# Gating the down weights instead of the sums in four modulated FFNs of a ten-stage fp32 block

## What is computed

```python
mod = (silu(c) @ w_mod[i] + b_mod[i]).reshape(-1, 3, 3, D)
h = modulate(x, norm_g[i, 0], mod[:, 0, 0], mod[:, 0, 1])
x = x + 0.5 * mod[:, 0, 2][:, None, :] * ((silu(h @ w_gate) * (h @ w_up)) @ w_down)
```

## Time and profile before

| | before |
|---|---|
| median of three runs | 2032.69 us |
| the profiled execution's own time | 2035.07 us |
| its span, first to last instruction | 2033.0 us |
| TensorE busy (matmul) | 1890.1 us, 93% |
| VectorE busy | 1424.8 us, 70% |
| ScalarE busy | 1173.2 us, 58% |
| HBM read | 371 MB, 183 GB/s over the span |
| granted TensorE clock, mean | 0.970 of full speed |

### The profile page before, as it was taken

One profiled execution on the slowest core, in us unless ns is written; L12 is line 12 of the kernel. 1 busy time (PEld: TensorE's weight loads), 2 busy tenths in 40 slices (PEclk: granted clock), 3 DMA queues, 4 the chain that ended last, 5 costly groups with the idle time before them and its releaser, 6 DMA issues.

```text
span 2033.0 us, 35938 instructions
## 1 busy us (share of the span) xinstructions
PE 1890.1 (93%) x14638; PEld 1737.6 (85%) x14638; DVE 1424.8 (70%) x2154; ACT 1173.2 (58%) x2049; POOL 12.9 (1%) x25
## 2 busy tenths in 40 slices
PE   6898899898989998999899999999989997889998
PEld 6887899887769997999889867899989996868998
DVE  5686877754667777877687676777787776565555
ACT  5544656664666556565576675555565555554332
POOL 0000000020000000000000000000000000000000
PEclk9999999989989998999999999899999998989999
DMA  8303666255057654888334403688778863124551
GB/s 318 115 4 120 221 231 238 94 188 186 23 182 252 238 212 165 324 290 286 131 136 162 150 1 121 252 289 287 242 263 291 285 228 125 53 93 156 187 187 52
DMA packets 96179, 374.96 MB, mean 184 GB/s; under 512 B 5776, under 2 KB 6416, under 8 KB 95248
## 3 DMA queue, kind: packets, MB, share of 16 engines
q1 hardware_dynamic: 95376, 372.15, 51.2%
q10 hardware_dynamic: 640, 0.52, 0.1%
HBM read 371.08 MB, written 1.05 MB: 183 GB/s over the span
## 4 chain that ended last, share of the span: by engine, by line
PE 84%; DVE 9%; ACT 5%; issue 2%; DMA 0%; ACTq 0%; DVEq 0%; SPq 0%
PE psum L997 36%; PE psum L1013 17%; PE psum L696 8%; PE psum L783 5%; PE psum L980 2%; PE psum L526 2%; DVE buf L597 2%; PE psum L1620 1%; PE psum L654 1%; DVE htok L2887 1%; PE psum L2997 1%; PE psum L3445 1%; PE psum L2505 1%; DVE x_res L490 1%; DVE htok L489 1%
## 5 line engine op out<-in xcount | busy, mean ns | idle before, releaser
L997 PEld LDWEIGHTS psum<-buf,buf 128*128 128x128 f32 x6048 | 741.9, 192 | 9.3
L997 PE MATMUL psum<-buf,buf 128*128 128x256 f32 x6048 | 745.7, 283 | 0.0
L1013 PE MATMUL psum<-buf,buf 128*128 128x512 f32 x1584 | 383.6, 391 | 2.2 <-DVE buf L1062 2.2
L1013 PEld LDWEIGHTS psum<-buf,buf 128*128 128x128 f32 x1584 | 289.2, 188 | 57.9 <-DVE buf L1062 3.0
L895 DVE TENSOR_TENSOR buf<-ring,buf 128x1024 fp32r<-128x1024 f32 x264 | 311.2, 1220 | 10.7 <-DVE modT L951 7.5
L889 ACT ACTIVATE buf<-ring 128x1024 fp32r<-128x1024 f32 x264 | 263.2, 1046 | 5.2 <-DVE buf L769 4.1
L696 PE MATMUL psum<-buf,buf 128*128 128x256 f32 x1944 | 245.9, 286 | 8.9 <-DVE buf L597 8.4
L696 PEld LDWEIGHTS psum<-buf,buf 128*128 128x128 f32 x1944 | 237.8, 192 | 14.6 <-DVE buf L597 13.1
L911 DVE TENSOR_TENSOR buf<-ring,buf 128x1024 fp32r<-128x1024 f32 x132 | 161.7, 1225 | 86.2 <-ACT buf L906 86.2
L906 ACT ACTIVATE buf<-ring 128x1024 fp32r<-128x1024 f32 x132 | 139.4, 1056 | 87.7 <-PE psum L1013 85.2
L597 DVE TENSOR_TENSOR buf<-ring,buf 128x1024 fp32r<-128x1024 f32 x97 | 118.7, 1232 | 92.6 <-ACT buf L591 85.3
(11 more groups left out here) (430 smaller groups left out, 2070.8 us busy)
## 6 DMA issues: line engine op xcount, KB each, us to landing
ring<-in_w_ffn SPq DMA_DIRECT2D x88, 1536.0 KB, 6.8
buf<-in_w_mod SPq DMA_DIRECT2D x144, 512.0 KB, 4.6
ring<-in_w_conv SPq DMA_DIRECT2D x44, 1536.0 KB, 6.5
ring<-in_w_ssd_in SPq DMA_DIRECT2D x16, 1536.0 KB, 6.4
ring<-in_w_hy_in SPq DMA_DIRECT2D x7, 1536.0 KB, 18.9
ring<-in_w_ns_in SPq DMA_DIRECT2D x7, 1536.0 KB, 7.4
ring<-in_w_ssd_out SPq DMA_DIRECT2D x5, 1536.0 KB, 6.6
ring<-in_w_cmp SPq DMA_DIRECT2D x4, 1024.0 KB, 5.2
```

The costliest lines, as they stand in the source:

```text
L997: ins = E.matmul(b[:, g * T:(g + 1) * T], w[:, wa, g, k, :], h[:, ha, k, :], start=k + n_ == 0, stop=k == KC - 1 and n_ == 2)
L1013: ins = E.matmul(acc[:, t, g * 512:(g + 1) * 512], hr[z][:, ha, t * P:(t + 1) * P], wd[z][:, wa, g * 512:(g + 1) * 512], start=j == 0 and ...
```

## The change

The gate is no longer multiplied into the sums. In the four modulated FFNs VectorE multiplies the raw down weights of each round by `rowb` (new function `gate_down`, into two new buffers `gated`), and the split works on the product. The row is made ahead of the first split. At the end VectorE only adds the sums to x. The cast of the hidden block goes from VectorE to ScalarE in these four FFNs. The conv FFNs are as they were. `pe_down` waits for `down_split` by name, and no longer for the row.

```diff
+        def add_plain(done):
+            ...
+                for t in range(NT):
+                    V.wait_ge(*done[t])
+                    added.append(dve.count(V.tensor_tensor(x[:, t, :], x[:, t, :], acc[:, t, :], ALU.add).then_inc(dve.sem, 1)))
...
+            gated = [Region(R_AT + 20480 + 4096 * u).take(CHUNK) for u in range(2)]
+            gated_at, high_at = {}, {}
...
+            def gate_down(j, row_point):
+                s, full = slot[j]
+                @block.vector
+                def _(_e):
+                    V.wait_ge(*full)
+                    V.wait_ge(*row_point)
+                    Ring.row_free = gated_at[j] = dve.count(V.tensor_tensor(gated[j % 2], slot_ap(s, SLOT)[:, 2 * CHUNK:], rowb[:, :],
+                                                                            ALU.mult).then_inc(dve.sem, 1))
...
             def split_down(j, free):
-                raw = slot_ap(s, SLOT)[:, 2 * CHUNK:]
+                raw = slot_ap(s, SLOT)[:, 2 * CHUNK:] if gate is None else gated[j % 2]
...
+                    if gate is not None:
+                        A.wait_ge(*gated_at[j])
                     Ring.p = act.count(A.activation(wd[j % 2][:, 0, :], raw, ACT.Copy).then_inc(act.sem, 1))
...
                     E.wait_ge(*hid[j])
-                    if j == 0 and gate is not None:
-                        E.wait_ge(*row_point)
+                    E.wait_ge(*down_split[j])
...
-                    vl(V.tensor_copy(hr[z][:, 0, :], hf[z]).then_inc(dve.sem, 1))
+                if gate is None:
+                    @block.vector
+                    def _(_e):
+                        vl(V.tensor_copy(hr[z][:, 0, :], hf[z]).then_inc(dve.sem, 1))
+                else:
+                    @block.scalar
+                    def _(_e):
+                        A.wait_ge(*mult[j])
+                        if j >= 2:
+                            A.wait_ge(*down[j - 2, 1])
+                        high_at[j] = act.count(A.activation(hr[z][:, 0, :], hf[z], ACT.Copy).then_inc(act.sem, 1))
+
+                @block.vector
+                def _(_e):
+                    if gate is not None:
+                        V.wait_ge(*high_at[j])
...
                 up_zero(h_pts)
+                if gate is not None:
+                    row_point = gate_row(mod_col(*gate, 2), 0.5, 0, [h_pts[-1]])
+                    gate_down(0, row_point)
                 split_down(0, [h_pts[-1]])
                 if gate is not None:
-                    row_point = gate_row(mod_col(*gate, 2), 0.5, 0, [h_pts[-1]])
+                    gate_down(1, row_point)
                 mod_products(0)
...
                     split_down(j, [down[j - 2, 1]] if j >= 2 else [h_pts[-1]])
+                    if gate is not None and j + 1 < NF:
+                        gate_down(j + 1, row_point)
...
-                add = add_normed if gate is None else add_gated
-                return add([down[NF - 1, 0], down[NF - 1, 1]], row_point), (bias if len(mods) else None)
+                ends = [down[NF - 1, 0], down[NF - 1, 1]]
+                return add_normed(ends, row_point) if gate is None else add_plain(ends), (bias if len(mods) else None)
```

More of the change, by code:

```diff
@@ L491, in add_gated @@
             return added
+        def add_plain(done):
+            added = []
+            @block.vector
[3 more added lines that the diff above has]
+                    added.append(dve.count(V.tensor_tensor(x[:, t, :], x[:, t, :], acc[:, t, :], ALU.add).then_inc(dve.sem, 1)))
+            return added
         def norm_transpose(gain, shift, added, parts, bias=None):
@@ L999, in _, with pe_down @@
                     up[j] = pe.count(ins.then_inc(pe.sem, 1))
-            def pe_down(j, row_point):
+            def pe_down(j):
                 z = j % 2
@@ L1096, in run @@
                     mod_sums(j - 1)
-                    pe_down(j - 1, row_point)
+                    pe_down(j - 1)
                     split_down(j, [down[j - 2, 1]] if j >= 2 else [h_pts[-1]])
+                    if gate is not None and j + 1 < NF:
+                        gate_down(j + 1, row_point)
                     if nxt is not None and j == NF - 4:
@@ L1109, in run @@
                     load_table(ACT.Sqrt)
-                pe_down(NF - 1, None)
+                pe_down(NF - 1)
                 def bias():
                     add_bias()
-                add = add_normed if gate is None else add_gated
-                return add([down[NF - 1, 0], down[NF - 1, 1]], row_point), (bias if len(mods) else None)
+                ends = [down[NF - 1, 0], down[NF - 1, 1]]
+                return add_normed(ends, row_point) if gate is None else add_plain(ends), (bias if len(mods) else None)
             return dict(load_a=load_a, load_b=load_b, pre_a=pre_a, pre_b=pre_b, run=run, gain=gain, shift=shift, h=h)
```

## The result

The changed kernel takes 2049.92 us in the median (2048.48 to 2053.63, four runs) against 2032.62 beside it: a ratio of 1.0090, 95% interval 1.0077 to 1.0103. It is slower by 17.3 us. The forecast was 2054, with a range of 2045 to 2067. A second set of runs beside the experiments gave 2051.96 against 2032.39, 1.0093 (1.0078 to 1.0108). The profiled execution took 2053.63 us, its span is 2051.5.

The account below looks back on a forecast made before the run. TensorE was taken as the bound, with 84% of the chain that ended last. Losses of 29.1 us less 8.2 gained gave net +20.9 on the median of 2032.69, forecast 2054 us, range 2045 to 2067.

Parts of the forecast that it names:

- The start: First rounds of each FFN: VectorE waits for the row, `up(2)` 7.1 us later in three FFNs, 2.8 in FFN 11.
- The round: Settled rounds with two side rows: VectorE's chain 8.47 us, taken as 8.50, equal to TensorE's; its slack falls to nothing.
- The tail: End of each FFN: one add per half without gate multiplies gains 2.2, 1.5, 2.2 and 2.35 us, 8.2 in all.
- The sum: All four FFNs: lost 9.3 + 8.5 + 8.5 + 2.8 = 29.1 us, gained 8.2, net +20.9.
- The signs of being wrong: Settled rounds: L1058 following L1058 by over 8.6 us, or TensorE waiting for VectorE in the middle of an FFN.
- The clock at the start: Rival: gaps at FFN starts lower TensorE's clock in `up(2)`, 0 to 3 us more, 2054 to 2057; no chance of its own.
- The long loop: Rival: VectorE's settled round exceeds TensorE's, priced at 8.65 to 8.70 us, 2064 us; range 2058 to 2076, chance 0.20.
- The faster case: Rival: FFN start costs under 2 us, `hid(0)` ready by about the end of `up(1)`; -8 us, 2024 to 2026, chance 0.03.

Follow-up runs that it names:

- e4: The kernel before with plain adds at the end and no gate applied in the four FFNs: 2021.39 us, ratio 0.9943.
- e5: The kernel before with only the cast of the hidden block moved to ScalarE, gate at the end: 2032.64 us, ratio 0.9999.
- e7: The changed kernel with one more VectorE copy of 256 columns behind each gate multiply: 2064.93 us, ratio 1.0166.
- e3: The changed kernel with gate(1) and round 0's side products moved behind round 0's multiply and subtraction: 2055.54 us, ratio 1.0110.
- e1: The changed kernel with the gate row made early, its 16 products in TensorE's gap ahead of the norm: 2032.25 us, ratio 1.0000.
- e8: The changed kernel with e1's early row, the cast back on VectorE and side products spread over rounds 2 to 21: 2012.37 us, ratio 0.9901.

## Why the prediction was right, and where it was off

*Direction and range*: right, and by the mechanism that was forecast.

*The start.* Forecast: `down(0)` at 812.4 and `up(2)` at 818.5. Measured: 813.20 and 819.38, in a profile in which `up(0)` began 0.88 us later than before; less that, 812.3 and 818.5. The loss to `up(2)` was put at 7.1 us in three FFNs and 2.8 in FFN 11; it is 7.14, 7.29, 7.03 and 2.75, which is 24.2 in all for 24.1.

*The round.* Forecast 8.47 by the sum, 8.50 taken. Measured 8.47 or 8.48; rounds with the bias instruction take 8.94 or 8.51, rounds with one side row 8.05. Over the 20 rounds from `mult(0)` to `mult(20)` the three FFNs take 169.7, 168.9 and 168.9 us where the sum gives 170.1, 169.3 and 169.3: 0.4 less in each. This is the term that was mis-sized. The last matmul ends later by 1.8, 1.0 and 0.9 us beyond the start's loss, where 2.2, 1.4 and 1.4 were forecast for `down(21)`; its waits are 1.01, 0.56 and 0.53 us.

*The tail.* 8.2 us forecast. From the end of the last matmul to the end of the last add it was 3.63, 4.19, 3.62 and 3.63 us; in the changed kernel it is 1.26, 3.15, 1.26 and 1.26, 8.1 less in all. The term for FFN 01, 1.5, came out as 1.04, and the others as 2.37, a little above the 2.2 taken for two of them. In e4 FFN 01 gives 2.5, and so its FFNs gain 9.5. The 1.8 us from there to the 11.3 of its median lie outside the FFNs, and the profile shows where 1.2 of them can be: the stretch from FFN 00 to FFN 01, with SSD, is 299.1 us for 300.3. The rest I did not resolve.

*The sum.* At the end of the last matmuls the changed kernel has lost 28.0 us, forecast 29.1; with the tail that is +19.9 us in the FFNs against 20.9. The median moved by 17.3 in one set and by 19.6 in the other. Of the profiled execution's +18.5 us of span, +0.9 came before FFN 00, and MLA with its norm gave back 2.4, with instructions that no edit touched; in e4 and e5 MLA kept its 155 us. That stretch before and after (the number behind the comma is TensorE's busy time; the third from the end is the granted clock):

```profile
1681.44:1836.82 155.38, 130.23 (x862) 113.57 (x863) 94.03 (x179) 88.99 (x184) 0.00 (x0) 0.90 0.25 89
...
1701.91:1854.89 152.98, 126.91 (x863) 111.20 (x863) 94.09 (x179) 89.15 (x185) 0.00 (x0) 0.92 0.25 90
```

So the 4 us between 2054 and 2050 are about 1 us of the sum and, for the rest, time of other stages, where the clock falls at other moments, and the spread of the medians. No term of the forecast stood for these.

*The signs of being wrong.* "TensorE waits for VectorE in the middle of an FFN" came true once, for 0.19 us at 836.81. "VectorE nearly without idle time" did not quite: in ten settled rounds of FFN 00 it is busy 73.3 of 84.8 us, 86%, and the rest are mostly its waits for ScalarE, such as the 0.48 us for the cast. The sum had these hand-overs in it, so the round is right all the same.

*The clock at the start*, a rival put at 0 to 3 us: it fell, as feared, but on `down(0)` (4.56, 5.39 and 4.61 us for 2.91 in FFN 00, 01 and 10), which a second wait swallowed; `up(2)` ran at full speed in all three (5.99 us). The prediction had placed it in `up(2)`, where it fell in e7; nothing in its sum said that it would be `down(0)`. e3 shows what it costs when nothing swallows it. The Trainium skill, "TensorE: Matmul & The Clock Gate" (§ HAM oscillation), says that bursts behind a long wait start slow each time. e3 agrees (8.45 us for 5.92 behind 6.14 us), and so do the three `down(0)` of the changed kernel. e1 agrees in FFN 00 (7.47 us) and not in FFN 01 and 10 (5.99 us behind 3.14 and 3.18 us).

*The long loop*, 0.20: did not happen; e7 shows how near it was: 0.2 us more per round cost their full price.

*The faster case*, 0.03: its condition was named rightly (gate(1) and side products must not stand ahead of `hid(0)`) but was not enough. e3 meets it and is the slowest but one: `up(2)` would not have followed in time, as the same work stands ahead of its split. It took the early row, the cast back and late side work together to leave TensorE no wait at the start (e8). The step that fails in this rival is "`up(2)` could follow in time".

## What to carry to other kernels

An engine with 30% of idle time can still have none where it counts: add up its work from start to start over one round, hand-overs to the other engines included, and compare that with the bound engine's round. When the two are equal, whatever is late at the start of a loop stays late to its end, so look at the first two rounds apart from the settled ones, and move side work out of them first. An edit that loses in its first form may be worth its whole forecast gain once nothing waits for its input.

## What the runs showed of the hardware

- The length of one gap of TensorE did not settle its clock afterwards. `up(2)` takes 5.92 to 5.99 us at full speed. Behind a gap of 6.14 us it took 8.45 and 8.70 (e3), behind 3.18 us 7.47 in one FFN and 5.99 in another (e1), and behind 1.79 us 7.47 (e7), where in the same place, also after a slow `down(0)`, it took 5.99 behind 1.63 us (changed kernel).
- Where the low clock falls matters as much as how long it lasts. On `down(0)` of the changed kernel, 4.56 us for 2.91, it cost nothing, as TensorE had to wait behind it; on `up(2)` of e3 it came out at the last add with 0.7 to 1.8 us per FFN.
- Ahead of the norm's transposes a gap of 2.45 us in place of 4.55 was mostly followed by four transposes in 0.66 us in place of 1.11, but not behind FFN 10 in e4 (1.11 us).
- A small VectorE instruction between two large ones costs less than its duration: 0.20 us from start to start for a copy that is busy for 0.29.
- The same stages with the same instructions differed by up to 5.3 us from kernel to kernel, in the first four stages, and the stretch with MLA by 2.5 us. For edits worth a few microseconds the distances inside the edited stage tell more than the span.
